# A decoder trunk on one core: three pieces of the hand-written order moved

## The reference

```python
xn = rmsnorm(h, norm_mix)                      # part 1: two token mixers, gated
q, k, v, cx, cb, cc, ga, gcv = split(xn @ w_in)          # w_in is 1024 x 8192
for each of 16 heads (width 64):               # stick-breaking attention, causal
    z = q k^T / 8 ;  log_stay = log_sigmoid(-z)
    w = exp(log_sigmoid(z) + sum over later keys of log_stay) ;  y_attn = w v
y_conv = cb * conv3(cc * cx)
h += (sig(ga) * (y_attn @ w_a) + sig(gcv) * (y_conv @ w_c)) @ w_out
xn = rmsnorm(h, norm_xattn)                    # part 2: 4 heads over 256 memory tokens
h += softmax(xn wq (rmsnorm(mem) wk)^T / 16) (rmsnorm(mem) wv) wo
xn = rmsnorm(h, norm_ffn)                      # part 3: product-key experts
per token, 8 heads: 16 best of 128 x 128 experts, gates = softmax of their scores
h += sum over the 128 chosen experts of gate * gelu(u[e] . xn) * v[e]   # u, v: 16384 x 1024
out = rmsnorm(h, norm_final)
```

## Time and profile before

| | |
|---|---|
| median of three runs | 2274.61 us (2273.43 to 2278.4) |
| the profiled execution: time / span | 2278.71 us / 2277.0 us |
| PE busy | 2040.5 us (90%), 9031 matmuls |
| DVE busy | 1199.9 us (53%) |
| ACT busy | 420.5 us (18%) |
| POOL busy | 910.1 us (40%) |
| DMA | 613.48 MB, mean 269 GB/s |
| mean granted TensorE clock | 0.925 of full |
| front of half 0 alone | 0 to 605 us |
| half 0's first expert indices ready | 562.8 us |
| front of half 1 on PE | 611 to 1236 us |
| dense gates and tables begin on DVE | 1283 us |

### The profile page before, as it was taken

The page is one execution under the profiler, slowest core; times in us unless marked ns, Lnnn a source line. Parts: engine busy times, 40 slices in busy tenths (PEclk is TensorE's granted clock), DMA queues, the critical chain, the costliest instruction groups (busy, mean ns, idle before and its releaser), DMA issues.

```text
span 2277.0 us, 24064 instructions
## 1 busy us (share of the span) xinstructions
PE 2040.5 (90%) x9031; PEld 1307.7 (57%) x9031; DVE 1199.9 (53%) x3046; ACT 420.5 (18%) x979; POOL 910.1 (40%) x785
## 2 busy tenths in 40 slices
PE   8999999989799998998888287899999887899997
PEld 7577886746685777884747254433333454333332
DVE  0122100013964887785748999944243999553301
ACT  2233210111212434111201022200000222100001
POOL 0000000000762334453426677844445888564522
PEclk9999999999899999999899578799999777999999
DMA  7322344324997777898858889999999999999976
GB/s 236 125 93 85 127 158 149 113 91 136 387 359 270 230 235 255 313 382 294 295 203 323 305 321 312 320 383 340 343 336 344 322 330 323 346 402 376 361 254 202
DMA packets 252440, 613.48 MB, mean 269 GB/s; under 512 B 18676, under 2 KB 121124, under 8 KB 252324
## 3 DMA queue, kind: packets, MB, share of 16 engines
q0 software_dynamic: 110592, 402.70, 49.4%
q1 hardware_dynamic: 141120, 208.17, 26.5%
q10 hardware_dynamic: 612, 1.07, 0.1%
HBM read 609.77 MB, written 2.10 MB: 269 GB/s over the span
## 4 chain that ended last, share of the span: by engine, by line
PE 71%; POOL 9%; DVE 9%; DMA 5%; issue 4%; ACT 2%; DVEq 0%; SPq 0%; POOLq 0%; ACTq 0%
PE ps L513 28%; PE ps L724 20%; PE ps L525 9%; PE ps L687 6%; POOL u_rows L475 5%; POOL v_rows L487 4%; DVE u_rows L1188 4%; PE ps L550 2%; PE ps L562 2%; PE ps L536 1%; DMA v_rows<-in_peer_v_dram,idx_turned 1%; DMA wring<-in_peer_w_query_dram 1%; PE ps L659 1%; ACT wbuf L848 1%; DMA wring<-in_w_branch_attn_dram 1%
## 5 line engine op out<-in xcount | busy, mean ns | idle before, releaser
L475 POOL DMA_INDIRECT u_rows<-in_peer_u_dram,idx x512 | 615.0, 1201 | 1044.9 <-DVE idx L1175 562.8
L1188 DVE CUSTOM_DVE_ANT_0 u_rows<-u_rows,xn 128x1024 f32<-128x1024 f32 x512 | 618.9, 1218 | 218.5 <-DMA u_rows<-in_peer_u_dram,idx 216.7
L513 PE MATMUL ps<-xT,wring 128*128 128x256 f32 x2560 | 579.1, 387 | 11.3 <-DVE xT L980 4.9
L513 PEld LDWEIGHTS ps<-xT,wring 128*128 128x128 f32 x2560 | 492.6, 194 | 81.8 <-DVE xT L980 4.9
L724 PE MATMUL ps<-d_rows,gates 128*128 128x512 f32 x1024 | 457.3, 599 | 0.0
L724 PEld LDWEIGHTS ps<-d_rows,gates 128*128 128x128 f32 x1024 | 189.3, 190 | 267.8 <-issue 267.8
L687 PE MATMUL ps<-v_rows,diag 64*64 64x512 f32 x2048 | 295.5, 700 | 32.7 <-DMA v_rows<-in_peer_v_dram,idx_turned 31.1
L487 POOL DMA_INDIRECT v_rows<-in_peer_v_dram,idx x128 | 146.9, 1148 | 265.2 <-PE ps L687 246.3
L714 PEld LDWEIGHTS ps<-hot_b,hot_a 128*128 128x128 f32 x1024 | 151.4, 235 | 128.0 <-DVE hot_b L1252 101.5
L714 PE MATMUL ps<-hot_b,hot_a 128*128 128x64 f32 x1024 | 161.1, 323 | 64.3 <-DVE hot_b L1252 64.3
L911 ACT ACTIVATE diag<-ident,wgt 128x64 f32<-128x64 f32 x256 | 75.8, 335 | 581.9 <-PE ps L687 528.9
(11 more groups left out here) (167 smaller groups left out, 1834.3 us busy)
## 6 DMA issues: line engine op xcount, KB each, us to landing
wring<-in_w_in_dram SPq DMA_DIRECT2D x128, 512.0 KB, 6.2
d_rows<-in_peer_v_dram SPq DMA_DIRECT2D x128, 512.0 KB, 6.7
wring<-in_peer_w_query_dram SPq DMA_DIRECT2D x32, 512.0 KB, 6.4
wring<-in_w_branch_conv_dram SPq DMA_DIRECT2D x16, 512.0 KB, 5.9
wring<-in_w_branch_attn_dram SPq DMA_DIRECT2D x16, 512.0 KB, 4.6
wring<-in_w_out_dram SPq DMA_DIRECT2D x16, 512.0 KB, 5.0
wring<-in_xattn_wq_dram SPq DMA_DIRECT2D x16, 512.0 KB, 4.6
wring<-in_xattn_wo_dram SPq DMA_DIRECT2D x16, 512.0 KB, 5.6
```

Source lines behind the costliest of these rows:

```text
L475: pool.indirect_dma_start(out=u_rows[:, n % URING, :], out_offset=None, in_=peer_u[0], in_offset=bass.IndirectOffsetOnAxis(ap=idx[:, g % I ...
L513: mm = pe.matmul(bank(job)[:, 0:HN], w[:, k % 4, P * b:P * (b + 1)], act[:, k, :], start=(k == 0), stop=(k == KT - 1))
L1188: dve.tensor_tensor_reduce(out=u, in0=u, in1=(xn2 if h else xn1)[:, i, :], scale=1.0, scalar=0.0, op0=ALU.mult, op1=ALU.add, accum_out=dot ...
```

## The change

Three moves; no operation is added or removed, nor is any size changed.

1. In `attention_units`, the unit `y` of head hd - 1 is listed right behind `z` of head hd + 1 and ahead of `c` of head hd; it was behind `wexp` of head hd.
2. In DVE's loop, pieces 5, 6 and 7 of the gelu are issued at steps 11, 12 and 13 of the group, not 5, 6 and 7, for groups whose step number lies in the first half (those of groups 0 to 14). ACT's Exp for them stays at step 5.
3. A new unit `n2a` holds ACT's part of `n2`. In half 0 it stands behind the first of the four pairs of memory keys; `n2` itself (PE's transposes, DVE's copies) stays behind all four. In half 1 it stands right ahead of `n2`. It has no cost in the table and no product of its own.

```diff
@@ attention_units
             if more:
                 units.append(("z", h, hd + 1))
+            if hd:
+                units.append(("y", h, hd - 1))
             units.append(("c", h, hd))
             if more:
                 units.append(("exln", h, hd + 1))
...
             units.append(("wexp", h, hd))
-            if hd:
-                units.append(("y", h, hd - 1))
@@ front_units
         if h == 0:
-            units += [("xk", h, p) for p in range(4)]
+            units += [("xk", h, 0)]
+        units += [("n2a", h, i) for i in range(HT)]
+        if h == 0:
+            units += [("xk", h, p) for p in range(1, 4)]
         units += [("n2", h, i) for i in range(HT)]
@@ scalar: front
-                elif kind == "n2":
+                elif kind == "n2a":
                     for c in range(2):
                         wait_taken(act, JOB[("wo", h, c)] + n)
-                    inverse_rms(unit, hbuf[:, tile, :], xnb[:, n, :])
-                    normed(unit, hbuf[:, tile, :], xnb[:, n, :])
+                    inverse_rms(("n2", h, n), hbuf[:, tile, :], xnb[:, n, :])
+                    normed(("n2", h, n), hbuf[:, tile, :], xnb[:, n, :])
@@ vector: main loop
-                if 0 < g <= GROUPS and e < 8:
+                late = 6 if g < HG else 0
+                if 0 < g <= GROUPS and e < 5:
                     gelu(g - 1, e)
+                if 0 < g <= GROUPS and 5 <= e - late < 8:
+                    gelu(g - 1, e - late)
```

## The result

The changed kernel took 2252.28 us (median of 4 runs, 2249.97 to 2254.14) against 2276.51 us before on the same chips (4 runs, 2273.43 to 2278.41): a ratio of 0.9894, 95% interval 0.9877 to 0.9912. It is faster by 24 us, 1.1%. The forecast was 36.6 us and 2238, with a range up to 2252. The measured time lies just outside the range. The side is right, the size is off by a third.

A forecast was written before the change was run, and what follows sets the result against it. PE was taken to bound most of the kernel, with DVE alone holding up two parts before 1283 us. 10.6 + 5.7 + 0.6 - 0.3 + 20 = 36.6 us off 2278.71, as a median 2238 us; range 2225 to 2252.

The forecast's parts named there:

- Move 1 in half 0: Attention of half 0: PE's waits for ACT's exponential before scores, last sums and last product go; gain 10.6 us.
- Move 3: Between memory keys and queries of half 0: gap shrinks by 4.6 us, half the low-clock loss goes, 1.1; sum 5.7 us.
- Move 1 in half 1: Attention of half 1: PE's waits for wbuf and lo and some low clock go; 20 us, between 0 and 30.
- rival (a): Attention of half 1: DVE paces it, lo late at most heads, 8 of 20 us remain; 2250 us, chance 0.17.
- PE-only sum: Attention of half 1: 15.0 us of wbuf waits, 4.4 of lo waits, 11 of low clock; 30 us for PE alone.
- limit by DVE: Attention of half 1: DVE needs 23.6 us per pair of heads against PE's 22.9, so PE cannot have all its gain.
- The term for the clock: Attention of half 1: of 15 us lost to low clock, perhaps 11 lie behind waits that can go.
- Move 2: Before DVE's first unit of half 1: 0.6 us gained; before the third norm, 0.3 lost; DVE's long Exp waits cost nothing.
- the collision: POOL's gathers in longer bursts beside weight loads may make PE wait for weights; taken as 0, bound 3 us.
- The signs named beforehand: First indices near 547 us, free banks amid memory keys, half 1 lo waits within 15 us, 1283 moved near 1246.
- (c): Attention of half 1: wbuf waits replaced one for one by lo waits; gain 16.6 us, 2258 us, chance 0.07.

The follow-up runs named there:

- the steps of before: Moves 1 and 3 without move 2, y's cost in the table given to wexp, against the kernel before: ratio 0.9808, 2239.21 us.
- one brake off: Moves 1 and 3 with late gelu pieces only at the first of the stretch's two groups, against the kernel before: ratio 0.9886.
- the first run: Moves 1 and 3 alone, the gelu's last pieces back at steps 5 to 7, against the kernel before: ratio 0.9847, 2241.24 us.

## Why the prediction was right or wrong

**Move 1 in half 0: right.** 10.6 us forecast, 9.7 found, by the mechanism named. **Move 3: right, a little small.** 5.7 us forecast; the stretches with the gap and with the query matmuls fell by 5.8 and 1.9 us. The query matmuls took 27.88 us, so the whole low clock went, not half of it, and the gap came to 3.2 us, less than the 4.35 of the kernel's start: there the 16 transposes took 3.28 us, here 2.04.

**Move 1 in half 1: right in size, and rival (a) was at work inside it.** Forecast 20 us between ends of 0 and 30; found 19.4. PE-only sum and limit by DVE were both there: with the steps of before, the same order gave 28.1 us (231.7 to 203.6), near the 30 that PE alone would give, so the 1.0 us between `max` and `lo` at each head cost 9 us. The sixteen waits sum to 16.3 us; PE's waits for `lo` fell from 11.3 to 4.1 us when they went. The term for the clock, 11 us, came to 7.5 in the changed kernel (PE busy for 188.3 us instead of 195.8) and to 10.1 with the steps of before. Its reading of the earlier trace rows was too simple, though: the sums that took 2.35 us also stood behind a wait of 1.07 us for the scores. What the slow ones at 752.39 had besides was a second wait right ahead of them, 0.59 us for `lo`. Most of the single waits of 1.07 us left the clock up.

**Move 2: wrong, and this is the step that failed.** The text said of DVE's 14.80 us wait in the stage of queries, keys and values: "There DVE runs ahead of PE and will wait at the next unit anyway, so I cost that at nothing; its cover is DVE's lead." For DVE that is true: it waited 47.9 us at the next unit. But a wait of DVE is also a wait of POOL (34.8 us in this stretch before, 6.1 after), and of the transfers POOL starts. The text did name the collision, "gathers come in longer bursts beside the weight loads", and then took 0 and set the bound at 3 us, beside DMA shares of 1.04 and 1.01 that are those of two other stretches (604 to 621 and 926 to 1042 us; this one had 0.96). Measured it is 14.4 us (9.5 of waiting, 4.9 of lower clock behind the waits); move 2 alone gave 12.6 us (99.7 against 87.1), and with the steps of before 14.9 (101.2 against 86.3). The bound had no row behind it. There was one to be had in the stage just ahead, where DVE and the gathers ran at full rate and the DMA share was already above 1. The chain of waits of the kernel before shows a load of weights there:

```profile
579.46 20.37 DMA wring<-in_peer_w_query_dram
```

An estimate from it: a ring of six buffers brings at most six loads in that time, one in 3.4 us. PE needs one in 3.45 us. While the gathers ran at their full rate, the ring had nothing to spare. In the changed kernel's stretch the chain shows two such loads, and PE's waits of 3.78 and 3.34 us behind them:

```profile
623.82 21.10 DMA wring<-in_w_in_dram
644.96 7.15 PE ps L516 x24
652.53 19.97 DMA wring<-in_w_in_dram
672.55 7.13 PE ps L516 x24
```

**The signs named beforehand.** The first expert indices came 13.7 us sooner (549.1 us instead of 562.8), not 16, since the start took 3.7 us longer. PE found its banks free amid the memory keys. Its waits for `lo` in half 1 were 10.2 us, under the 15 named, and the stage took 198.5 us as forecast. The one-hots began at 1263 us and not near 1246, mostly for the 14.4 us of the stretch and the 3.7 of the start.

**The rest.** The saving carried through to the end without loss, as forecast; a last 4 us came on top that the change does not explain. No rival as worded came true. The measured time fell between (a) and (c) for a reason that neither named. Without the 14.4 us the changed kernel would stand at 2238 us, the forecast to the microsecond, but that closeness would be luck in part: move 3 gave 2 us more than its term, the last stretch 4 more and the start 3.7 less.

## What to carry to other kernels

A wait that costs its own engine nothing can be the throttle of a transfer that competes with the critical one; before removing it, ask what will be issued sooner, on which queue, and whether the DMA engines have room in that very stretch. Where steps are derived from costs along a list, moving an entry moves the steps of everything behind it: here this put two dependent operations side by side, for 9 us. And when a new order has let an engine off, look again for what now waits, since the second gain (a number in a table) was 9 us beside the 31 of the first.

## What the runs showed of the hardware

Gathers and weight loads shared the DMA engines unevenly. In the first 58 us of the changed kernel's stretch, with the DMA share at 1.04 and 391 GB/s, the median 0.5 MB weight load took 17.4 us to landing, the median gather of the same size 8.0. Over the whole stretch the loads went from 7.9 to 13.1 us, while the gathers' median hardly moved (7.8 to 8.0 us for 33 of them). The median of a stretch is a rough sign, for it mixes the full part with the empty one: with one brake off it was 7.3 us, and PE still waited 6.3 us for weights.

The price of starvation was half as much again as the waits themselves in the changed kernel: 9.5 us of waiting came with 4.9 us of slower matmuls, granted clock 0.94 instead of 0.98. It was not the same everywhere. With move 2 alone, 10.0 us of waits came with 3.2 us more of PE's busy time (88.7 against 85.5); with one brake off, 6.3 us came with 5.1 (91.2 against 86.1 in the first run).

Why the stretch from the first gather to the first query matmul took 61 to 62 us on one chip and 55 to 59 on two others was not tried.
